# A fused encoder layer on one core: the loads of x at the start spread over SyncE's and ScalarE's DMA queues

## What is computed

```python
def layer(x, p, lb, state, segments):
    h = rmsnorm(x, p['norm_pre'])          # x * rsqrt(mean(x*x, -1) + EPS) * g, row by row
    proj = h @ p['w_in']
    ...                                    # mLSTM, HGRN2 and RWKV-7 branches
    merged = ga * (ya @ p['w_proj_a']) + gb * (yb @ p['w_proj_b']) + gc * (yc @ p['w_proj_c'])
    y = merged @ p['w_out']
    return x + rmsnorm(y, p['norm_post']), state
```

## Time and profile before

| | us |
|---|---|
| median of 3 runs | 2247.14 (2247.12 to 2247.55) |
| the profiled execution, its own time | 2246.83 |
| its span, first to last instruction | 2245.0 |
| TensorE busy | 2211.7 (99%) |
| VectorE / ScalarE / GpSimd busy | 1330.0 / 782.9 / 57.4 |
| start of the first product | 26.28 |

### The profile page before, as it was taken

One profiled execution on the slowest core, in us unless ns is written; L12 is line 12 of the kernel. 1 busy time (PEld: TensorE's weight loads), 2 busy tenths in 40 slices (PEclk: granted clock), 3 DMA queues, 4 the chain that ended last, 5 costly groups with the idle time before them and its releaser, 6 DMA issues.

```text
span 2245.0 us, 44631 instructions
## 1 busy us (share of the span) xinstructions
PE 2211.7 (99%) x18925; PEld 2159.5 (96%) x18925; DVE 1330.0 (59%) x2080; ACT 782.9 (35%) x1196; POOL 57.4 (3%) x87
## 2 busy tenths in 40 slices
PE   6999999999999999999999999999999999999998
PEld 5999999999999999999999999999999999999997
DVE  5434434388776777677565655656656664454354
ACT  5311212234333333334242433333333353344343
POOL 0000001000000000000000000000000000000000
PEclk9999999999999999999999999999999999999999
DMA  5322222132333333333121212113221354344465
GB/s 189 133 71 96 78 90 89 55 124 98 135 119 128 110 127 121 126 118 138 39 95 39 75 59 75 58 54 126 90 71 60 106 183 159 140 157 169 148 211 184
DMA packets 67065, 249.35 MB, mean 111 GB/s; under 512 B 9050, under 2 KB 16396, under 8 KB 50068
## 3 DMA queue, kind: packets, MB, share of 16 engines
q1 hardware_dynamic: 66916, 247.14, 31.6%
HBM read 216.92 MB, written 30.19 MB: 110 GB/s over the span
## 4 chain that ended last, share of the span: by engine, by line
PE 98%; DMA 1%; DVE 0%; SPq 0%; ACT 0%; issue 0%; DVEq 0%; POOL 0%; ACTq 0%; POOLq 0%
PE acc L1001 53%; PE acc L1191 15%; PE branch L1191 8%; PE acc L1575 7%; PE branch L1575 2%; PE branch L1281 1%; PE branch L1481 1%; PE branch L1297 1%; PE branch L1306 1%; DMA scratch<-in_x_all 1%; PE acc L1044 1%; PE branch L1136 1%; PE branch L1129 0%; PE branch L1271 0%; PE branch L1349 0%; PE branch L1595 0%
## 5 line engine op out<-in xcount | busy, mean ns | idle before, releaser
L1001 PE MATMUL acc<-act_hi,w_hi 128*128 128x320 f32 (+2 forms) x2912 | 887.8, 305 | 0.0
L1001 PE MATMUL acc<-act_lo,w_hi 128*128 128x320 f32 (+2 forms) x2912 | 863.3, 296 | 0.0
L1001 PE MATMUL acc<-act_hi,w_lo 128*128 128x320 f32 (+2 forms) x2912 | 863.0, 296 | 0.0
L1001 PEld LDWEIGHTS acc<-act_hi,w_hi 128*128 128x128 f32 x2912 | 548.3, 188 | 12.8 <-issue 5.0
L1001 PEld LDWEIGHTS acc<-act_lo,w_hi 128*128 128x128 f32 x2912 | 548.4, 188 | 0.7
L1001 PEld LDWEIGHTS acc<-act_hi,w_lo 128*128 128x128 f32 x2912 | 548.1, 188 | 0.0
L2109 DVE TENSOR_TENSOR w_lo<-w_raw,w_hi 128x2048 fp32r<-128x2048 f32 x121 | 277.1, 2290 | 248.8 <-ACT w_hi L1633 245.3
L1633 ACT ACTIVATE w_hi<-w_raw 128x2048 fp32r<-128x2048 f32 x122 | 233.6, 1915 | 134.7 <-PE branch L1575 119.5
L1191 PE MATMUL acc<-corner_terms,w_hi 128*128 128x288 f32 x736 | 148.1, 295 | 0.0
L1191 PE MATMUL acc<-act_hi,w_hi 128*128 128x288 f32 x496 | 146.6, 296 | 0.0
L1191 PE MATMUL acc<-act_lo,w_hi 128*128 128x288 f32 x496 | 146.4, 295 | 0.0
(11 more groups left out here) (459 smaller groups left out, 3437.2 us busy)
## 6 DMA issues: line engine op xcount, KB each, us to landing
w_raw<-in_w_stream SPq DMA_DIRECT2D x124, 1024.0 KB, 4.8
w_raw<-in_w_stream SPq DMA_DIRECT2D x92, 512.0 KB, 5.7
gate_logits<-gate_out SPq DMA_DIRECT2D x48, 288.0 KB, 2.3
scratch<-gate_logits SPq DMA_DIRECT2D x48, 288.0 KB, 5.3
scratch<-in_x_all SPq DMA_DIRECT2D x9, 512.0 KB, 7.5
branch_rows<-branch_out SPq DMA_DIRECT2D x16, 288.0 KB, 2.3
scratch<-in_x_all SPq DMA_DIRECT2D x3, 1024.0 KB, 10.8
out_y_prompt<-scratch SPq DMA_DIRECT2D x6, 512.0 KB, 2.9
```

The lines of the kernel that those rows point to most:

```text
L1001: last = mm(acc[s][:, at:at + hi - lo], a[:, s, w], b[:, k, lo:hi], start=(k == order[0] and a is whi and b is xh), stop=(k == order[-1] a ...
```

## The change

The vectors, the second half of tile 0, the constants and both pieces of tile 4 are asked for by ScalarE, ahead of its table load; SyncE keeps the first half of tile 0, tiles 1 to 3, the weights and the masks. On ScalarE's queue the order is: tile 0's second piece, constants, tile 4's two pieces, vectors. ScalarE's wait for the vectors moves from ahead of the first Square to behind the last.

```diff
@@ SyncE
-            sp.dma_start(vecs[:, :], vecs_in).then_inc(vecs_here, 16)
-            for t in range(5):
-                for a, b, src in given(t, ROWS[t]):
-                    sp.dma_start(xt[a:b, t, :], src).then_inc(x_here[t], 16)
-                if t == 0:
-                    sp.dma_start(full[:, :], full_in).then_inc(consts_here, 16)
+            for t in range(4):
+                a, b, src = given(t, ROWS[t])[0]
+                sp.dma_start(xt[a:b, t, :], src).then_inc(x_here[t], 16)
             for n in range(2):
                 sp.dma_start(wraw[:, n, :], w_stream[n]).then_inc(w_here[n], 16)
             sp.dma_start(masks[:, :], masks_in).then_inc(masks_here, 16)
@@ ScalarE
+            for t in (0, 4):
+                for a, b, src in given(t, ROWS[t])[t == 0:]:
+                    act.dma_start(xt[a:b, t, :], src).then_inc(x_here[t], 16)
+                if t == 0:
+                    act.dma_start(full[:, :], full_in).then_inc(consts_here, 16)
+            act.dma_start(vecs[:, :], vecs_in).then_inc(vecs_here, 16)
             nc.scalar.preload_act_table_set("exp_and_others")
             S = S0["setup_scalar"]
-            act.wait_ge(vecs_here, 16)
             act.wait_ge(*S0["setup_pool"].after(0, "zeros"))
             for t in range(5):
                 r = ROWS[t]
...
                 f(x_junk[0:r, :], xt[0:r, t, :], ACT.Square, accum_out=small[0:r, t:t + 1]).then_inc(x_sums, 1)
+            act.wait_ge(vecs_here, 16)
             act.wait_ge(w_here[0], 16)
```

## The result

| | before | changed |
|---|---|---|
| median of 20 runs each, us | 2247.02 (2245.63 to 2248.89) | 2250.20 (2247.86 to 2252.95) |
| ratio, 95% interval | | 1.0015 (1.0008 to 1.0022) |
| profiled execution, its time / span | 2246.83 / 2245.0 | 2250.86 / 2249.0 |
| last Square starts | 21.54 | 23.96 |
| first product starts | 26.28 | 29.66 |

The forecast was 2246.3 us in a range up to 2249.6; the median lies outside it. The sign is that of the first rival, the size twice its. All but 0.6 us of the 4.0 us between the two profiled spans is there when the first product starts.

What follows compares the result with a forecast made beforehand. TensorE is busy 99% of the span, so only the first product's start, set by the x loads, counts. Terms -0.45 - 2.4 + 0 + 2.0 = -0.85 us gave 2246.3 us, range 2243.0 to 2249.6.

Steps and rivals of the forecast that it cites:

- first rival: Loads at the start: transfers on the two queues serialize, no overlap is won; +1.55 us, 2248.7 us, chance 0.27.
- Term 1: Vectors leave the head of SyncE's queue: everything behind comes 0.45 us earlier; the vectors' later arrival costs nothing.
- Terms 5 and 6: ScalarE's five DMA issues ahead of its table load cost nothing; the weight and mask loads stay hidden.
- term 2: First tile's two halves, on two queues, move together at the full rate: -2.4 us.
- Term 4: Arrival order turns round: tile 3 lands last with two Squares behind it, so the last starts one pitch later, +2.0 us.
- Term 3: Last tile and constants move to ScalarE's queue: between 0 and -2.1 us, taken as 0.
- third rival: Tile 4's rows alternate with full tiles' and drag tile 2 to half rate, without overlap: +4.05 us, 2251.2 us, chance 0.06.
- The clock: TensorE's rise from 1.2 to 2.4 GHz after the first product may shift: +-1 us on every case.

Runs made afterwards that it cites:

- e4: Changed kernel with tile 4's two pieces back on SyncE's queue behind tile 3; median 2246.49 us, ratio 0.9997 to the kernel before.
- e8: Kernel before with the vectors asked for behind tile 4 on SyncE's queue and ScalarE's wait for them behind the Squares; 2249.10 us, ratio 1.0006.
- e7: Kernel before with tiles 0 and 4 in one load each and the vectors alone issued by ScalarE; 2243.88 us, ratio 0.9985.
- e9: Changed kernel with VectorE's wait for the vectors moved behind its scalings; 2249.28 us, ratio 1.0008 to the kernel before.
- e2: Changed kernel with all four engines taking the tiles in the order 0, 1, 4, 2, 3; 2250.52 us, ratio 1.0015 to the kernel before.
- e3: Changed kernel with the vectors first on ScalarE's queue and tiles taken in the order 0, 1, 4, 2, 3; 2249.76 us, ratio 1.0009 to the kernel before.
- e10: Changed kernel's two queues with tiles 0 and 4 one load each, VectorE's wait for the vectors behind its scalings; 2245.40 us, ratio 0.9993 to the kernel before.

## Why the prediction was wrong

**What held.** The bound: a microsecond at the first product is a microsecond of the kernel. Term 1: about -0.6 us by tile 0's start (8.72 against 9.30), e4 and e8 (-0.65 to -0.7 on the last Square), where 0.45 was forecast; but only with the vectors off the front of every queue (e7: nothing). Terms 5 and 6: the table load, done at 5.3 us, waited for nothing and held up nothing, and ScalarE found the first weight tile there. And the change stayed under 0.2%, as the prediction had it with 0.89 (1.0015, though its interval reaches 1.0022).

**The step that failed first is term 2,** "I take -2.4 us, since the halves have nothing in common but the engines and their issues now start side by side". It was nothing: tile 0 was there 0.58 us earlier, no more than term 1 gave. The bounds were right and the wrong end was taken. The rows were read rightly (half the rows take twice the time per byte), but the first rival's mechanism held, and more strongly than told, since the halves weren't even in turns: one queue moved at 214 GB/s and then the other at 217. With term 2 at nothing the prediction's own sum is +1.55 us and its sign that of the result.

**The second is term 1's last sentence, "Nothing for this"**, for the vectors. They landed at 21.6 us in the first profile, 5.6 later than the latest time considered, because they stood behind tile 4, which itself landed only at 18.9. The reasoning counted VectorE's own time and left out what its catching up does to others: it stretches GpSimd's operations on the very chain that ends last, here tile 4's mean from 0.19 to 1.15 us. Last Square to first product took 5.70 instead of 4.74 us: +0.96, and in e8, where it is worst, +2.4 (mean and power both). Removing the wait gave 0.9 us on the median (e9; less than its interval).

**Term 4 had the right place and only a part of the picture.** In the first profile its signs came: a wait of 5.85 us ahead of tile 2's Square, tile 4 in before tile 3, the last two Squares one pitch (2.10 us, where 2.0 was taken) apart. But it blamed the order, and e2 and e3 show that another order wins nothing: taking turns delays the tile of the first queue that has a neighbour (tile 2 to 19.16 us from 14.35), lands the rest bunched, and leaves two to four Squares behind each other. The last Square came 2.42 us later than before; -0.45 + 2.0 would have been 1.55, and the remaining 0.9 is tile 3's later landing, 21.86 where 21.54 - 0.45 = 21.09 was implied, and 0.1 of the pitch. **Term 3 at nothing** was therefore too kind by about 0.8 us: the third rival (the slow half drags the full tiles down) is real at a third of its price.

**The clock** was to add a microsecond either way. In the first profile it rose some 2 us later relative to the product and cost about 1.1 us, for a reason that stays open.

Adding up for the profiled pair, spans 2245.0 and 2249.0: last Square +2.42, from it to the product +0.96, from the product to the end +0.62 (the clock's 1.1 less some 0.5 us by which the stretch behind the last products was shorter), together +4.0. The median's +3.2 lies between that and the milder course. Only one of the 20 timed executions was under 2249 us (2247.86), so the milder course seems the rarer; two executions were profiled, too few to say.

## What to carry to other kernels

Before spreading loads over two queues, ask who uses them in which order: here the same engines served both (239 GB/s for two queues in turns, 417 for full tiles on one), so that what was gained in one tile was taken from its neighbour, and the in-order consumer found everything late and at once. Look instead at the rate of each load in the trace; where a 64-row one goes at half of a 128-row one, as here, join the two in one load. And a small table at the end of a queue is late by everything ahead of it; let its wait stand directly ahead of the first instruction that reads it.

## What the runs showed of the hardware that was not expected

- The two halves of tile 0, issued at 0.73 and 0.74 us on two queues, moved strictly one behind the other (q1 to 4.3 us and q10 from 4.6 in one execution, q10 first in another), while later loads of the same queues took turns (102 and 100 packets from 11 to 17 us). Being the first load of a queue isn't the reason: in e10 the constants, first on theirs, moved beside tile 0 from the start (0.06 and 0.53 MB from 2 to 4 us). What is, is open.
- The turns are not the same in every execution: the constants, issued at 1.37 and 1.35 us in two executions of one program, landed at 12.2 and 8.3 us. With one queue, two executions agreed to 0.3 us.
- GpSimd's 80x1 power took 0.55 us beside an idle VectorE and 2.30 us under its scalings, and its 80x1 mean 0.19 and 1.15 us, ending 0.05 us behind the scaling.
